# Output projection as seven half-size block products instead of one full product

## The chip, the cores and the metric

The kernel runs on one core of one Trainium2 chip. The metric is the device time of one execution in microseconds (us). The kernel before took 826.01 us as the median of 3 runs (825.94 to 826.08).

## The reference, cut to what matters

One transformer-like block on `x` of 512 rows by 2048 columns in fp32. The change touches the last line only; the rest explains what fills the engines before it.

```python
h    = rms_norm(x, norm_w)
proj = h @ w_in                                  # 2048 x 6144: q, k, v, gate_a, pool input, gate_p
attn = diff_attention(q, k, v, ...)              # 8 heads, two softmaxes each
pool = multiscale_pool(u_p, w_pool, pool_scale)  # four window sizes
mixed = concat([attn * silu(g_a), pool * silu(g_p)])   # 512 x 2048
x = x + mixed @ w_out                            # w_out is 2048 x 2048
```

## The kernel before, in words

The kernel feeds TensorE (PE) each fp32 factor as two `float32r` parts, a high one (ScalarE, ACT, copies and rounds) and a low one (VectorE, DVE, subtracts the high part from the fp32 value). A product is three matmuls: high*high, low*high, high*low (`products`, line 292 issues every one of them, so all have one line in the profile).

The first part of the kernel runs four rounds over the input projection with attention and pooling threaded between its 48 half-units a round. What it leaves in `mixed` is the transposed result: 16 k-tiles of 128 partitions (the contraction index) by 512 columns (the rows of x). The last values of `mixed` are written by DVE at lines 810 (head) and 836 (pool, announced by `pool_mixed`).

The output projection walks four column chunks of 512 of `w_out`. In a chunk each of 16 k-tiles is one "half" of 128x512 weights. SP loads two halves with one DMA into one of four slots of `raw` (`load_out`, line 181). ACT writes the high part of a half into one of four slots of `w_hi` (`split_high`, line 483, waits until PE has used the half four before, `w_used`), DVE writes the low part (`split_low`, line 669). PE then runs 12 matmuls on the half: four row tiles of x times three products, into four PSUM banks; two sets of four banks alternate between chunks. `mixed` itself is split once, a k-tile at a time, by ACT line 520 and DVE line 700, into `h_hi` and `h_lo`. After a chunk DVE adds the residual x (line 856, `add_x`) and SP stores the result (lines 249 to 262). The last four tiles are stored one at a time.

Every engine takes its instructions in the order of the program, so a wait on one holds all that follow on that engine. GpSimd (POOL) does nothing after its one broadcast at the start (line 269).

## Time and profile before

| what | value |
|---|---|
| median of 3 runs | 826.01 us (825.94 to 826.08) |
| span of the profiled execution | 824.4 us |
| PE busy | 802.7 us, 97% |
| DVE busy | 468.4 us, 57% |
| ACT busy | 364.6 us, 44% |
| POOL busy | 2.5 us |
| mean granted TensorE clock | 0.995 of full speed |
| DMA | 89.12 MB, mean 108 GB/s |

The profile covers one execution from its first to its last instruction (the span); the run's time is 1.6 us longer than the span. Busy shares of PE count overlapping pipelined matmuls, so the distance between the starts of matmuls says more than their durations. A line with "idle before" says how long the engine stood still ahead of such instructions and which engine released it.

### The profile page before, as it was taken

Reading aid. Unit: us, or ns where it says so; the run is one execution under the profiler, and the core shown is the slowest. Engines: PE = TensorE matmul, PEld = TensorE weight load, DVE = VectorE, ACT = ScalarE, POOL = GpSimd, SP = SyncE. Lnnn points to the kernel's source line nnn. Section 1 sums busy time; section 2 is a strip of 40 time slices with the busy share of each in tenths; the row PEclk is TensorE's granted clock in tenths of the full one; section 3 lists DMA queues with packets and bytes.
Section 4 is the critical chain, followed back from the end, with each engine's and each line's share of the span. In section 5 each row is a group of like instructions: output and inputs, shape, how many; then the busy total and the mean of one; then the engine's idle time right before and its main releaser. Section 6 shows DMA issues by size and latency. Waiting matters only on the chain.

```text
span 824.4 us, 10257 instructions
## 1 busy us (share of the span) xinstructions
PE 802.7 (97%) x3616; PEld 662.8 (80%) x3616; DVE 468.4 (57%) x694; ACT 364.6 (44%) x590; POOL 2.5 (0%) x5
## 2 busy tenths in 40 slices
PE   3799999999999999999999999999999999999998
PEld 3688888888888888888888888888888888888886
DVE  5628775772686667428775672686668643232322
ACT  6544445542454634454346543454644542222220
POOL 1000000000000000000000000000000000000000
PEclk9899999999999999999999999999999999999999
DMA  9233622213244222233622223254212464424331
GB/s 339 82 103 102 179 77 78 69 59 127 76 127 129 74 76 76 77 101 102 178 76 76 76 70 108 81 144 130 66 63 77 128 204 153 146 88 148 102 102 51
DMA packets 69525, 89.12 MB, mean 108 GB/s; under 512 B 4481, under 2 KB 53889, under 8 KB 68993
## 3 DMA queue, kind: packets, MB, share of 16 engines
q1 hardware_dynamic: 67632, 86.72, 33.8%
q10 hardware_dynamic: 1874, 2.18, 0.9%
q8 instruction: 9, 0.15, 0.1%
q14 instruction: 10, 0.08, 0.0%
HBM read 78.39 MB, written 4.19 MB: 100 GB/s over the span
## 4 chain that ended last, share of the span: by engine, by line
PE 96%; DVE 2%; ACT 1%; DMA 1%; issue 0%; DVEq 0%; ACTq 0%
PE ps L292 94%; PE ps L382 2%; DVE mixed L663 1%; DVE h_lo L653 1%; DMA mixed<-in_x 1%; ACT at_hi L468 0%; PE ps L354 0%; DVE mixed L856 0%; PE ps L284 0%; ACT h_hi L461 0%; ACT x_rms L471 0%; DVE x_rstd L662 0%; DVEq L852 0%; DVEq L661 0%; ACTq L466 0%
## 5 line engine op out<-in xcount | busy, mean ns | idle before, releaser
L669 DVE TENSOR_TENSOR w_lo<-raw,w_hi 128x512 fp32r<-128x512 f32 x256 | 175.5, 690 | 300.4 <-ACT w_hi L483 297.8
L483 ACT CAST w_hi<-raw 128x512 fp32r<-128x512 f32 x256 | 158.7, 622 | 374.0 <-PE ps L292 373.0
L292 PE MATMUL ps<-h_hi,w_hi 128*128 128x512 f32 x768 | 303.0, 395 | 1.8 <-DVE h_lo L653 1.8
L292 PE MATMUL ps<-h_lo,w_hi 128*128 128x512 f32 x768 | 300.4, 391 | 0.0
L292 PE MATMUL ps<-h_hi,w_lo 128*128 128x512 f32 x768 | 205.9, 390 | 0.0
L292 PEld LDWEIGHTS ps<-h_hi,w_hi 128*128 128x128 f32 x768 | 144.8, 189 | 31.8 <-ACT w_hi L483 2.2
L292 PEld LDWEIGHTS ps<-h_hi,w_lo 128*128 128x128 f32 x768 | 144.4, 188 | 30.6
L292 PEld LDWEIGHTS ps<-h_lo,w_hi 128*128 128x128 f32 x768 | 144.9, 189 | 29.6
L292 PE MATMUL ps<-w_hi,h_hi 128*128 128x512 f32 x256 | 99.7, 389 | 0.0
L292 PE MATMUL ps<-w_hi,h_lo 128*128 128x512 f32 x256 | 99.6, 389 | 0.0
L292 PE MATMUL ps<-w_lo,h_hi 128*128 128x512 f32 x256 | 99.6, 389 | 0.0
L292 PEld LDWEIGHTS ps<-w_hi,h_hi 128*128 128x128 f32 x256 | 48.1, 188 | 10.1 <-issue 0.3
L292 PEld LDWEIGHTS ps<-w_lo,h_hi 128*128 128x128 f32 x256 | 48.1, 188 | 10.0
L292 PEld LDWEIGHTS ps<-w_hi,h_lo 128*128 128x128 f32 x256 | 48.1, 188 | 10.0
L591 ACT ACTIVATE probs<-ps,neg_max 128x512 f32<-128x512 f32 x64 | 43.6, 691 | 0.0
L777 DVE TENSOR_REDUCE row_max<-ps 128x2 f32<-128x1024 f32 x32 | 38.9, 1217 | 0.0
L784 DVE TENSOR_TENSOR at_lo<-ps,at_hi 128x512 fp32r<-128x512 f32 x32 | 21.9, 684 | 10.0 <-ACT at_hi L584 10.0
L284 PE MATMUL ps<-ident,mixed 128*128 128x128 f32 x64 | 10.5, 330 | 15.8 <-DVE mixed L663 15.7
L292 PE MATMUL ps<-kh_twice,q_stack 128*128 128x512 f32 x64 | 25.4, 397 | 0.0
L292 PE MATMUL ps<-kl_twice,q_stack 128*128 128x512 f32 x64 | 24.9, 390 | 0.0
L765 DVE SCALAR_TENSOR_TENSOR probs<-probs,coef 128x512 f32<-128x512 f32 x32 | 24.0, 752 | 1.1
L584 ACT CAST at_hi<-ps 128x512 fp32r<-128x512 f32 x32 | 18.7, 583 | 10.5 <-PE ps L292 10.5
(105 smaller groups left out, 584.3 us busy)
## 6 DMA issues: line engine op xcount, KB each, us to landing
raw<-in_w_in SPq DMA_DIRECT2D x96, 512.0 KB, 3.6
raw<-in_w_out SPq DMA_DIRECT2D x32, 512.0 KB, 3.8
mixed<-in_x SPq DMA_DIRECT2D x8, 1024.0 KB, 6.9
out<-mixed SPq DMA_DIRECT2D x3, 1024.0 KB, 6.5
kh_twice<-kh_twice SPq DMA_DIRECT2D x8, 256.0 KB, 5.3
kl_twice<-kl_twice SPq DMA_DIRECT2D x8, 256.0 KB, 6.0
q_stack<-v_hi SPq DMA_DIRECT2D x8, 256.0 KB, 3.6
wp_raw<-in_w_pool ACTq DMA_DIRECT2D x4, 256.0 KB, 3.3
```

Of the source, the lines that this page charges most:

```text
L284: last = nc.tensor.transpose(ps[:, bank + i // 4, (i % 4) * P:(i % 4 + 1) * P], x_rows[:, t, (8 * b + i) * P:(8 * b + i + 1) * P], ident[: ...
L292: last = nc.tensor.matmul(dst, lhs, rhs, start=first and i == 0, stop=final and i == len(pairs) - 1, skip_group_check=True)
L382: last = nc.tensor.transpose(ps[:, TB, t * P:(t + 1) * P], probs[:, 0, t * P:(t + 1) * P], ident[:, :])
L483: nc.scalar.copy(w_hi[:, h % W_SLOTS, :], raw[:, unit % RAW_SLOTS, part * 512:part * 512 + 512]).then_inc(w_hi_ready, 1)
L584: nc.scalar.copy(at_hi[:, :, t * P:(t + 1) * P], ps[:, TB, :].rearrange("p (t s) -> p t s", t=ST)).then_inc(at_hi_ready, 1)
L591: nc.scalar.activation(probs[:, c, :], ps[:, S0 + c, :], ACT.Exp, bias=neg_max[:, c:c + 1], scale=SCALE, accum_out=row_sum[:, c:c + 1]).th ...
L653: nc.vector.tensor_tensor(h_lo[:, 8 * b:8 * b + 8, t * P:(t + 1) * P], ps[:, bank:bank + 2, :].rearrange("p b (k s) -> p (b k) s", s=P), h ...
L663: nc.vector.scalar_tensor_tensor(out=x_rows[:, t, :], in0=x_rows[:, t, :], scalar=x_rstd[:, t:t + 1], in1=norm_row, op0=ALU.mult, op1=ALU. ...
L669: nc.vector.tensor_tensor(w_lo[:, h % W_SLOTS, :], raw[:, unit % RAW_SLOTS, part * 512:part * 512 + 512], w_hi[:, h % W_SLOTS, :].bitcast( ...
L765: nc.vector.scalar_tensor_tensor(out=probs[:, 0, :], in0=probs[:, 1, :], scalar=coef[:, :], in1=probs[:, 0, :], op0=ALU.mult, op1=ALU.add) ...
L777: chain(nc.vector.reduce_max(row_max[:, :], ps[:, S0:S0 + 2, :], AX_X))
L784: nc.vector.tensor_tensor(at_lo[:, :, t * P:(t + 1) * P], ps[:, TB, :].rearrange("p (t s) -> p t s", t=ST), at_hi[:, :, t * P:(t + 1) * P] ...
```

## The change

The product is cut in 2x2 blocks: `mixed` in A(row, col) with 256 rows of x and 1024 of the contraction, `w_out` in B(row, col) of 1024 by 1024. Seven block products ("passes") replace the eight of the plain scheme. A pass has 8 k-tiles of weights 1024 columns wide, each taken in two halves of 512 columns, and 2 row tiles: 6 matmuls a half, 16 halves a pass, 112 halves in all.

| pass | form of A (left factor) | weights | banks |
|---|---|---|---|
| 0 | A00 | B00 (`wide`, plain load) | set 0, fresh |
| 1 | A10 - A11 | B00+B01 (`wide` += ) | set 1, fresh |
| 2 | A01 | B10 (`tall`, plain load) | set 0, added to pass 0 |
| 3 | A00 - (A10 - A11) | B00+B01+B11 (`wide` +=) | set 1, added to pass 1 |
| 4 | A00 - A10, in place | B01+B11 (`tall` load, then +=) | set 0, fresh |
| 5 | A01 - (A00 - A10 + A11) | B11 (`tall`, plain load) | set 1, fresh |
| 6 | A11 | B00+B01+B10+B11 (`wide` +=) | set 0, added to pass 4 |

The sums of weights are made by 32 DMAs of 512 KB that POOL issues with an accumulate operation (`accum_op`): they add a block of `w_out` in HBM to what lies in SBUF. Each waits until DVE has made the low part of that tile for the pass before. The sums of A are 16 `tensor_tensor` of 128x512 on POOL; another 12 on POOL add a shared corner term to the x blocks, or subtract it. SP makes 32 plain loads of `w_out` tiles of 512 KB, as before (8 `wide`, ahead of the passes, and 24 `tall`, within them), four loads of x blocks of 1 MB, three block stores of 1 MB and four of 256 KB. ACT and DVE split each of 112 halves, and each form of A in four pairs of k-tiles (28 pairs, 128x512 each; 16 before). ACT copies pass 0's banks once (4 instructions), DVE reads banks 24 times (16 before). To make room the buffers lie at fixed offsets in one arena: `tall` over the attention buffers, `wide_b` over `at_hi` and `at_lo`, the x blocks over the upper halves of `h_hi` and `h_lo`, `corner` and `form_sum` over `work`.

The added lines at the core of the diff; the removed ones are the loops told of above (lines 229 to 263, 425 to 449 and 848 to 865):

```diff
+        PASS_SET = (0, 1, 0, 1, 0, 1, 0)
+        PASS_FRESH = (True, True, False, False, True, True, False)
+        PASS_WIDE = (True, True, False, True, False, False, True)
+        PASS_LANDED = (16, 16, 16, 32, 16, 48, 48)
 ...
+            for h in range(PASSES * P_HALVES):
+                p, hj = divmod(h, P_HALVES)
+                j, part = divmod(hj, 2)
+                slot = h % W_SLOTS
+                if hj == 0 and p == 1:
+                    pe.wait_ge(evacuated, ROUNDS * 4 + START)
+                    pe.wait_ge(pool_mixed, ROUNDS * 2 + START)
+                if j % 2 == 0 and part == 0:
+                    pe.wait_ge(form_lo_ready, (KP // 2) * p + j // 2 + 1)
+                pe.wait_ge(w_lo_ready, IN_HALVES + h + 1)
+                for i in range(2):
+                    b = 2 * part + i
+                    bank = OUT_BANKS[PASS_SET[p]][b]
+                    if j == 0 and p == 2:
+                        pe.wait_ge(first_copied, b + 1)
+                    if j == 0 and p >= 3:
+                        pe.wait_ge(bank_read, 4 * (p - 3) + b + 1)
+                    hi, lo = form_tile(h_hi, p, j, i), form_tile(h_lo, p, j, i)
+                    last = products(ps[:, bank, :],
+                                    [(hi, w_hi[:, slot, :]), (lo, w_hi[:, slot, :]), (hi, w_lo[:, slot, :])],
+                                    j == 0 and PASS_FRESH[p], j == KP - 1)
+                    if j == KP - 1 and i == 0:
+                        last.then_inc(bank_done, 1)
+                last.then_inc(w_used, 1)
 ...
+            def form_high(p, pair):
+                if p == 0:
+                    act.wait_ge(w_used, IN_HALVES - G_HALVES + 2)
+                    act.wait_ge(head_mixed, 2 * pair + 2 + START)
+                elif p == 1:
+                    act.wait_ge(w_used, IN_HALVES - G_HALVES + 4)
                 else:
+                    act.wait_ge(w_used, p_halves(p - 2, KP - 1, 1))
+                if p == 2 or p == 6:
+                    act.wait_ge(pool_mixed, ROUNDS * 2 + START)
+                elif p > 0:
+                    act.wait_ge(form_summed, (KP // 2) * (0, 0, 0, 1, 2, 3)[p] + pair + 1)
+                nc.scalar.copy(form_pair(h_hi, p, pair), form_fp32(p, pair)).then_inc(form_hi_ready, 1)
+            def split_form_w(h):
+                p, hj = divmod(h, P_HALVES)
+                j, part = divmod(hj, 2)
+                if part == 0:
+                    act.wait_ge((wide_in, wide_added, tall_in, wide_added, tall_added, tall_in, wide_added)[p][j],
+                                PASS_LANDED[p])
+                act.wait_ge(w_used, IN_HALVES + h - W_SLOTS + 1)
+                nc.scalar.copy(w_hi[:, h % W_SLOTS, :], w_tile(p, j)[:, part * 512:part * 512 + 512]
+                               ).then_inc(w_hi_ready, 1)
 ...
+            form_high(0, KP // 2 - 1)
+            for h in range(W_SLOTS, PASSES * P_HALVES):
+                p, hj = divmod(h, P_HALVES)
+                split_form_w(h)
+                if hj in (4, 7, 10, 13) and p + 1 < PASSES:
+                    form_high(p + 1, (hj - 4) // 3)
+                if p == 1 and hj in (2, 3):
+                    for b in (2 * hj - 4, 2 * hj - 3):
+                        wait_bank(act, 0, b)
+                        nc.scalar.copy(corner_part(b), ps[:, OUT_BANKS[0][b], :]).then_inc(first_copied, 1)
 ...
+            def read_bank(p, b):
+                wait_bank(dve, p, b)
+                bank = ps[:, OUT_BANKS[PASS_SET[p]][b], :]
+                if p == 1 and b == 0:
+                    dve.wait_ge(x_part_in[2], 16)
+                if p == 2 and b == 0:
+                    dve.wait_ge(x_part_in[0], 16)
+                if p == 3:
+                    dve.wait_ge(first_copied, b + 1)
+                if p >= 4:
+                    dve.wait_ge(x_summed, 4 * (p - 4) + b + 1)
 ...
+            form_low(0, KP // 2 - 1)
+            for h in range(W_SLOTS, PASSES * P_HALVES):
+                p, hj = divmod(h, P_HALVES)
+                split_form_low(h)
+                if hj in (4, 7, 10, 13) and p + 1 < PASSES:
+                    form_low(p + 1, (hj - 4) // 3)
+                if p >= 2 and hj in (2, 3):
+                    for b in (2 * hj - 4, 2 * hj - 3):
+                        read_bank(p - 1, b)
+            for b in range(4):
+                read_bank(PASSES - 1, b)
 ...
+            sp.wait_ge(head_done, ROUNDS * 2)
+            for j in range(RAW_SLOTS, KP):
+                load_wide(j)
+            sp.wait_ge(pool_done, ROUNDS)
+            sp.wait_ge(w_used, IN_HALVES)
+            for p in range(PASSES):
+                for j in range(KP):
+                    if p == 0 or p == 1:
+                        if j % 2 == 1:
+                            sp.wait_ge(w_lo_ready, p_halves(p, j, 1))
+                            load_tall(4 * p + j // 2, 1, 0)
+                        if j == 2:
+                            load_x(1 - p, 0)
+                        if p == 1 and j == 6:
+                            load_x(1, 1)
+                    if p == 2:
+                        sp.wait_ge(w_lo_ready, p_halves(p, j, 1))
+                        load_tall(j, 0, 1)
+                    if p == 3 and j == 0:
+                        load_x(0, 1)
+                    if p == 3 and j == 2:
+                        store(0, 0, 2)
+                    if p == 4:
+                        sp.wait_ge(w_lo_ready, p_halves(p, j, 1))
+                        load_tall(j, 1, 1)
+                    if p == 5 and j == 2:
+                        store(1, 1, 4)
+                    if p == 6 and j == 2:
+                        store(0, 1, 5)
 ...
+            def add_wide(p, j, row, col):
+                pool.wait_ge(w_lo_ready, p_halves(p, j, 1))
+                pool.dma_start(w_tile(0, j), w_block(row, col, j), accum_op=ALU.add).then_inc(wide_added[j], 16)
+            for j in range(KP):
+                add_wide(0, j, 0, 1)
+                if j == 0:
+                    pool.wait_ge(pool_mixed, ROUNDS * 2 + START)
+                    pool.wait_ge(head_mixed, ROUNDS * 2 + START)
+                if j % 2 == 0:
+                    pair = j // 2
+                    nc.gpsimd.tensor_tensor(sum_of(pair), block_of(1, 0, pair), block_of(1, 1, pair), ALU.subtract
+                                            ).then_inc(form_summed, 1)
+            for j in range(KP):
+                add_wide(1, j, 1, 1)
+            for pair in range(KP // 2):
+                pool.wait_ge(form_lo_ready, KP // 2 + pair + 1)
+                nc.gpsimd.tensor_tensor(sum_of(pair), block_of(0, 0, pair), sum_of(pair), ALU.subtract
+                                        ).then_inc(form_summed, 1)
+            for pair in range(KP // 2):
+                nc.gpsimd.tensor_tensor(block_of(1, 0, pair), block_of(0, 0, pair), block_of(1, 0, pair), ALU.subtract
+                                        ).then_inc(form_summed, 1)
+            for j in range(KP):
+                pool.wait_ge(tall_in[j], 32)
+                pool.dma_start(tall[:, j, :], w_block(1, 1, j), accum_op=ALU.add).then_inc(tall_added[j], 16)
+            for pair in range(KP // 2):
+                pool.wait_ge(form_lo_ready, 3 * (KP // 2) + pair + 1)
+                nc.gpsimd.tensor_tensor(sum_of(pair), block_of(0, 1, pair), sum_of(pair), ALU.subtract
+                                        ).then_inc(form_summed, 1)
+            for j in range(KP):
+                add_wide(3, j, 1, 0)
+            for row, col in ((1, 1), (0, 1), (1, 0)):
+                pool.wait_ge(x_part_in[2 * row + col], 16)
+                if (row, col) == (1, 0):
+                    pool.wait_ge(bank_read, 4)
+                for b in range(4):
+                    pool.wait_ge(bank_read, 8 + b + 1)
+                    nc.gpsimd.tensor_tensor(x_part(row, col, b), x_part(row, col, b), corner_part(b),
+                                            ALU.subtract if row > col else ALU.add).then_inc(x_summed, 1)
```

## Rows read from the trace of the kernel before

**Rows 1.** The page: busy time, its share of the span, instructions of each engine.
```profile
PE 802.7 (97%) x3616; PEld 662.8 (80%) x3616; DVE 468.4 (57%) x694; ACT 364.6 (44%) x590; POOL 2.5 (0%) x5
```

**Rows 2.** The chain that ended last, shares of the span by engine and line.
```profile
PE 96%; DVE 2%; ACT 1%; DMA 1%; issue 0%; DVEq 0%; ACTq 0%
PE ps L292 94%; PE ps L382 2%; DVE mixed L663 1%; DVE h_lo L653 1%; DMA mixed<-in_x 1%; ACT at_hi L468 0%; PE ps L354 0%; DVE mixed L856 0%; PE ps L284 0%; ACT h_hi L461 0%; ACT x_rms L471 0%; DVE x_rstd L662 0%; DVEq L852 0%; DVEq L661 0%; ACTq L466 0%
```

**Rows 3.** Groups by line, 644 to 820 us (count | busy us, mean ns | idle before).
```profile
L292 PE MATMUL ps<-w_hi,h_hi 128*128 128x512 f32 x256 | 99.7, 389 | 0.0
L669 DVE TENSOR_TENSOR w_lo<-raw,w_hi 128x512 fp32r<-128x512 f32 x62 | 42.9, 691 | 106.6 <-ACT w_hi L483 106.6
L483 ACT CAST w_hi<-raw 128x512 fp32r<-128x512 f32 x61 | 38.0, 622 | 120.7 <-PE ps L292 120.7
```

**Rows 4.** Timeline of PE, first and late output matmuls (start us, duration us).
```profile
645.98 0.47 PE L292 MATMUL ps<-w_hi,h_hi 128*128 128x512 f32 x1
...
811.99 0.39 PE L292 MATMUL ps<-w_hi,h_hi 128*128 128x512 f32 x1
...
818.79 0.39 PE L292 MATMUL ps<-w_hi,h_hi 128*128 128x512 f32 x1
...
819.93 0.39 PE L292 MATMUL ps<-w_lo,h_hi 128*128 128x512 f32 x1
```

**Rows 5.** Timeline of DVE and SP at the end.
```profile
818.38 2.66 DVE L856 TENSOR_TENSOR mixed<-ps,mixed 128x512 f32<-128x512 f32 x4 [7.56 <-PE ps L292]
819.10 2.31 SPq L261 DMA_DIRECT2D out<-mixed  x4
```

**Rows 6.** Timeline of DVE where the projection starts.
```profile
645.97 0.69 DVE L700 TENSOR_TENSOR h_lo<-mixed,h_hi 128x512 fp32r<-128x512 f32 x1
646.57 0.69 DVE L669 TENSOR_TENSOR w_lo<-raw,w_hi 128x512 fp32r<-128x512 f32 x1
647.18 1.40 DVE L836 SCALAR_TENSOR_TENSOR mixed<-ps,p_scale,work 128x512 f32<-128x512 f32 x2
```

**Rows 7.** Timeline of ACT where the projection starts.
```profile
643.77 0.61 ACT L520 CAST h_hi<-mixed 128x512 fp32r<-128x512 f32 x1
644.29 0.62 ACT L483 CAST w_hi<-raw 128x512 fp32r<-128x512 f32 x1
644.81 1.02 ACT L621 ACTIVATE work<-ps 128x1024 f32<-128x1024 f32 x1
```

**Rows 8.** POOL's arithmetic in the whole trace, by line (count | busy us, mean ns | idle before).
```profile
L269 POOL PARTITION_BROADCAST work<-work x1 | 2.3, 2293 | 2.1 <-DMA work<-in_norm_w 2.1
L915 POOL MEMSET const-float32-1.0<- 128x1 f32 x1 | 0.1, 99 | 0.0
```

**Rows 9.** SP's issues of w_out loads: ns min/median/max, first and last start.
```profile
L181 SPq DMA_DIRECT2D raw<-in_w_out x32: 367/372/383, 611.5 to 789.1; - x32
```

**Rows 10.** Stretches: us, busy us of PE, PEld, DVE, ACT, POOL; granted clock, DMA share, GB/s.
```profile
6.00:12.00 6.00, 1.09 (x5) 1.10 (x6) 3.63 (x4) 4.46 (x6) 0.00 (x0) 1.00 1.01 424
649.70:655.10 5.40, 5.40 (x25) 4.50 (x24) 2.59 (x4) 2.24 (x5) 0.00 (x0) 1.00 0.86 275
```

**Rows 11.** DMA issues by line (queue, count, KB each, median us from issue to landing).
```profile
raw<-in_w_out SPq DMA_DIRECT2D x32, 512.0 KB, 3.8
kh_twice<-kh_twice SPq DMA_DIRECT2D x8, 256.0 KB, 5.3
```

**Rows 12.** Stretches after PE's idle time near the start, columns as in rows 10.
```profile
26.00:28.00 2.00, 0.30 (x2) 0.00 (x0) 2.00 (x3) 1.67 (x3) 0.00 (x0) 0.50 0.00 0
28.00:30.00 2.00, 1.88 (x5) 1.50 (x6) 2.00 (x3) 1.67 (x2) 0.00 (x0) 0.50 0.00 0
```

**Rows 13.** Timeline of PE in the second of these stretches.
```profile
29.57 0.63 PE L292 MATMUL ps<-h_lo,w_hi 128*128 128x512 f32 x1
30.00 0.63 PE L292 MATMUL ps<-h_hi,w_hi 128*128 128x512 f32 x1
```

More of the change, by code:

```diff
@@ new lines, in hybrid_block, with fixed @@
+        at0 = -(-nc.sbuf_base // 64) * 64
+        sb("arena", [P, at0 - nc.sbuf_base + ARENA], U8)
+        place = [at0]
+        def fixed(name, shape, dt=F32, at=None):
+            offset = place[0] if at is None else at
+            size = 4
+            for n in shape[1:]:
+                size *= n
+            if at is None:
+                place[0] += size
+            return nc.alloc_sbuf_tensor_at(name, shape, dt, offset=offset), offset
+        h_hi, h_hi_at = fixed("h_hi", [P, KT, SEQ], F32R)
@@ L767, in dve_round @@
                                                        op0=ALU.mult, op1=ALU.add).then_inc(attn_ready, 1)
-                    split_low(m + 3, r)
+                    if last_round and m + 3 >= HALVES:
+                        split_form_low(m + 3 - HALVES)
+                    else:
+                        split_low(m + 3, r)
                     if m in (40, 45):
```

231 lines of the change are left out of this document (112 added, 119 removed).

## The prediction

> **What bounds the kernel now.** I read the page's busy times first. PE is at work 97% of the span, DVE 57%, ACT 44%, POOL is empty [rows 1]. Busy PE is not yet bound PE, so the chain of waits comes next: 94% of the time that leads to the end is one line, 292, the matmuls [rows 2]. The groups of the projection's stretch then say who waits for whom: ACT stood idle 120.7 us for PE and DVE 106.6 us for ACT, while the matmuls show no idle time [rows 3]. So PE alone sets the pace of the output projection, and everything else has room there.
>
> What one matmul costs is read from starts, not durations, because they overlap: from 811.99 to 818.79 there are 30 starts, so 6.80 / 30 = 0.2267 us each. The whole projection agrees: 768 matmuls start from 645.98 to 819.93, 173.95 / 767 = 0.2268 us [rows 4]. Its weights are loaded beside it; each matmul of the new scheme has the same shape and the same pair of load and product, so I keep 0.2267. For DVE and ACT the distance of starts counts too: 646.57 - 645.97 = 0.60 us on DVE [rows 6] and 644.29 - 643.77 = 0.52 us on ACT [rows 7] for a 128x512 operation.
>
> **What is removed.** 768 matmuls become 7 x 16 x 6 = 672. The 96 that go are worth 96 x 0.2267 = 21.8 us, all on the path. A half now lasts 6 x 0.2267 = 1.36 us and a pass 16 halves, 21.8 us.
>
> **ACT and DVE.** A pass asks ACT for 16 splits and 4 forms, 20 x 0.52 = 10.4 us (pass 1 has 4 copies more, 12.5). It asks DVE for 16 + 4 + 4 bank reads, 24 x 0.60 = 14.5 us. Both fit in 21.8. The splits run up to four halves ahead: half h is split when h-4 is done, about 1.1 us later it is ready, and PE wants it three halves (4.1 us) after the start of that; the lead is 3 us. Cost 0; PE's pace hides it. With that cover gone (a DVE held for over 3 us) each us shows in full.
>
> **Start and end.** The round before is unchanged, and the four plain `wide` tiles loaded as late as the last attention product are first split some 10 us later: 0. At the end the last four banks are read by DVE one after the other and stored in four DMAs of 256 KB as before: DVE's four reads begin at 818.38, beside the last matmuls, and the issues follow at 819.10 [rows 5]. The new last half ends bank by bank in the same way; 0, at most 0.7 us either way (a row tile more or less behind PE).
>
> **The sums of A on POOL: the chain through pass 0.** This is the place where a wait is added. ACT takes the form of pass 1 pair by pair after halves 4, 7, 10 and 13 of pass 0, in order, and holds all later weight splits until POOL has made the pair's sum. POOL makes it in order too, between its DMA issues: sum 1 stands behind the add of tile 2, sum 2 behind tile 4, sum 3 behind tile 6, and each add waits until DVE has finished that tile's second half (halves 5, 9, 13). So a ring closes: split, DVE, POOL issue I, POOL sum S, ACT form, split. In us from PE's first output matmul: the last pool values are there at 2.6 (line 836 starts at 647.18 and takes 1.40 [rows 6]). Half 5 is ready at 2.6 + S + 0.52 + 0.52 + 0.60; half 9 I + S + 3 x 0.52 + 0.60 later; half 13 I + S + 4 x 0.52 + 0.60 later; half 14 I + S + 2 x 0.52 + 0.60 later. Sum: 2.6 + 4S + 3I + 11 x 0.52 + 4 x 0.60 = 10.7 + 4S + 3I, and some 12 hand-overs that I estimate at 0.1 us each, 11.9 + 4S + 3I. PE wants half 14 at 14 x 1.36 = 19.0. Loss: 4S + 3I - 7.1.
>
> The trace shows neither S nor I. For S the ends are DVE's 0.60 us of the same shape [rows 6] and POOL's one real instruction, 2.29 us for a much larger output [rows 8]; I take the middle, 1.5. For I they are SP's issue, 0.37 us [rows 9], and again 2.29 us of POOL work for software that prepares one DMA; I take 1.0, nearer to SP's, since it is the same kind of job. Loss 6.0 + 3.0 - 7.1 = 1.9 us; ends 0 and 4 x 2.29 + 3 x 2.29 - 7.1 = 8.9.
>
> Later forms have a pass of slack: the sums for pass 3 start when the last add of pass 1 is issued, some 4 us ahead of pass 2, and are wanted one by one from 1.4 us into it. But in pass 2 POOL makes eight sums in a row.
>
> **POOL beside DVE.** Nothing runs on POOL in the projection now, so the trace shows no case of the two at once [rows 8], and from the rows alone each might run at its own pace: cost 0. If they exclude one another, pass 2 has 8 x 1.5 + 14.5 = 26.5 us of work for 21.8 plus the lead of 3, a loss of 1.7; other passes have 6 + 14.5 = 20.5, none. I take 0.6. By the Trainium skill, "SBUF — State Buffer", section "Who interferes with whom", a VectorE instruction with two SBUF inputs (the low parts are such) and a GpSimd one that reads SBUF keep each other out for the whole instruction; by that rule the sum would carry the 1.7 instead, and no run here shows it yet.
>
> **The accumulating DMAs.** The traffic of the projection grows by 32 x 512 KB. Plain price: at full use of the DMA engines the trace moves 424 GB/s [rows 10], so 512 KB take 1.25 us; the old loads of 2 KB rows reached 275 GB/s at a share of 0.86, or 320 GB/s, 1.6 us [rows 10]. The new rows are 4 KB, so 1.25. Within the passes: 24 `tall` loads 30 us, x blocks 4 x 2.5 = 10, two of the stores 5 by the time the last weights are due: 45 us. The 32 adds cost 32A. The last tile is due at about 6 x 21.8 + 19.0 - 4 = 146 us, so the queues keep up as a whole up to A = 101 / 32 = 3.15; up to the last tile of pass 4, 24A + 32.5 against 4 x 21.8 + 15 gives 2.9. No row shows an accumulating DMA. Lower end: the plain 1.25 us. Upper ends: 3.8 us if a DMA's whole issue-to-landing time repeated one by one, and 5.3 us, that of an SBUF-to-SBUF copy of half the size [rows 11]. An add must read both HBM and SBUF and write once, so I take twice the plain load, 2.5 us: nothing is late, cost 0. By the Trainium skill, "Collectives: The Full Stack", section "The bandwidth ceiling: the fold count and why AG ≠ RS ≠ AR", a DMA reduction runs at about half a copy's rate (ratio 1.93) because of its second source read; an estimate by it is 2.4 us, and the sum stays.
>
> **Sum.** Span 824.4 - 21.8 + 1.9 + 0.6 = 805.1 us. The runs last 1.6 us more than the span, so 806.7; I say 807. The median (826.01) and the span plus 1.6 are the same number here. Own range with small errors of each term: 804 to 812.
>
> **Rivals.**
> A. The adds are slow, and the DMA engines become the bound. For it: 16.8 MB of read-modify-write by an operation that no row prices, ends of 3.8 and 5.3 us. Against: nothing but the argument of two reads. Price: the work past 146 us shows, 45 + 32A - 146. It eats the gain of 19.3 at A = 3.76, the point from which the kernel is slower. At 4.55 (the middle of the upper ends) 44.6 us late: 826 - 19.3 + 44.6 = 851. At 5.3: 875. Place: waits of ACT's w_hi on the added tiles from pass 1 or 3 on, worst in passes 5 and 6. POOL's queue makes it worse, if issues wait for earlier ones to drain: the x sums that DVE needs in pass 5 stand behind the last eight adds.
> B. POOL is slow (S 2.29, I 1.6) but DMAs keep up. For it: software on the path. Against: only one instruction of it in the trace. Ring of pass 0: 9.2 + 4.8 - 7.1 = 6.9. Exclusion in pass 2: 18.3 + 14.5 - 24.8 = 8.0. Together 14.9, so 826 - 21.8 + 14.9 = 819; stalls of over 2 us may also cost clock: after idle time near the start PE was granted 0.50, its 1.2 GHz level [rows 12], and matmuls started 0.43 us apart [rows 13], so 4 us at that level lose 1.9 us.
> C. Both small losses meet and the gain is gone, 825 to 828.
>
> **Chances.** Forecast 0.50, B 0.20, A 0.25, C 0.05. What a measurement can tell from no change is about 0.2%, 1.7 us. Faster: forecast and B, 0.70; C is mostly within, 0.03; slower A and the rest, 0.27. The range for 8 in 10 begins at 803 (no loss at all is 804 and a little for the tail) and reaches through B to the milder half of A, 840; the likeliest case alone is 804 to 812.
>
> **What would show it.** The changed profile should have 3520 matmuls of the same 0.23 us distance, so a projection of about 155 us. Right about pass 0: idle time of ACT at the form copies (form_high) on POOL of 1 to 3 us each, and of PE before half 14. Right about the adds: issue-to-landing times near 4 to 6 us, no idle time of w_hi on a DMA. Wrong: landings over 10 us, DMA share near 1 for most of the projection, ACT waiting on `raw` or `tall` (rival A); POOL busy over 15 us a pass, or DVE's distances grown while POOL works (rival B). The prediction fails if A is over 3.8 us, or if POOL's sum and issue together take over 5.

## The result, and the profile after

The changed kernel took 832.97 us (median of 4, 831.21 to 837.57) where the kernel before took 825.98 (median of 4, 825.86 to 826.08): a ratio of 1.0093, 95% interval 1.0074 to 1.0113. It is 0.9% slower. I had forecast 807, faster with a chance of 0.7. The profiled execution is the longest of the four, 837.57 us with a span of 835.7: 11.3 more than before, where the medians differ by 7.0. What follows accounts for that one execution, and the sizes of its terms are its own.

The page's busy times come first, to stand against [rows 1], then its chain (against [rows 2]) and three of its DMA lines (count, KB each, median us from issue to landing):

```profile
PE 787.1 (94%) x3520; PEld 647.2 (77%) x3520; DVE 541.1 (65%) x762; ACT 401.7 (48%) x654; POOL 65.6 (8%) x65
...
PE 89%; DVE 6%; issue 2%; ACT 1%; POOL 1%; DMA 0%; ACTq 0%; DVEq 0%
...
tall<-in_w_out SPq DMA_DIRECT2D x24, 512.0 KB, 8.0
raw<-in_w_out POOLq DMA_DIRECT2D x12, 512.0 KB, 12.8
wide_b<-in_w_out POOLq DMA_DIRECT2D x12, 512.0 KB, 18.9
```

The 96 matmuls are gone (3520, as foreseen), but PE's share of the chain fell from 96% to 89% and DVE's rose from 2% to 6%. DVE has 72.7 us more of busy time for 68 more instructions: far more than 0.6 us each (0.6 would make 41 us). The groups of the projection, 646 to 830 us, show where (against [rows 3]; the low parts are line 867 now):

```profile
L424 PE MATMUL ps<-w_hi,h_hi 128*128 128x512 f32 x222 | 88.7, 399 | 24.9 <-DVE w_lo L867 17.2 <-issue 7.7
L867 DVE TENSOR_TENSOR w_lo<-tall,w_hi 128x512 fp32r<-128x512 f32 x48 | 56.8, 1192 | 18.1 <-ACT w_hi L670 17.5
L670 ACT CAST w_hi<-tall 128x512 fp32r<-128x512 f32 x48 | 29.9, 623 | 52.5 <-PE ps L424 52.5
```

PE, which stood idle nowhere in [rows 3], now waits 24.9 us, mostly for DVE's low part, whose mean went from 691 to 1192 ns. ACT's split is unchanged (622 and 623) and waits for PE, not for a DMA. A mean hides what kind of slowness it is, so the timelines of POOL and DVE are laid beside each other at the two longest stops. POOL in pass 2 (start us, duration us):

```profile
693.82 0.87 POOL L362 DMA_DIRECT2D wide_b<-in_w_out  x1 [1.73 <-DVE w_lo L867]
694.38 5.32 POOL L378 TENSOR_TENSOR form_sum<-mixed,form_sum 128x512 f32<-128x512 f32 x4
699.33 5.22 POOL L381 TENSOR_TENSOR mixed<-mixed 128x512 f32<-128x512 f32 x4
```

DVE in the same stretch:

```profile
692.76 0.69 DVE L867 TENSOR_TENSOR w_lo<-wide_b,w_hi 128x512 fp32r<-128x512 f32 x1 [0.61 <-ACT w_hi L670]
694.18 12.13 DVE L867 TENSOR_TENSOR w_lo<-tall,w_hi 128x512 fp32r<-128x512 f32 x3 [0.72 <-ACT w_hi L670]
```

PE in the same stretch:

```profile
697.12 0.39 PE L424 MATMUL ps<-w_lo,h_hi 128*128 128x512 f32 x1
705.21 0.77 PE L424 MATMUL ps<-w_hi,h_hi 128*128 128x512 f32 x1 [7.70 <-issue]
705.77 0.63 PE L424 MATMUL ps<-w_hi,h_lo 128*128 128x512 f32 x1
706.20 0.63 PE L424 MATMUL ps<-w_lo,h_hi 128*128 128x512 f32 x1
```

POOL in pass 4:

```profile
753.97 0.87 POOL L362 DMA_DIRECT2D wide_b<-in_w_out  x1 [1.49 <-DVE corner L1033]
754.53 10.17 POOL L400 TENSOR_TENSOR x_right<-x_right,corner 128x512 f32<-128x512 f32 x8
764.38 5.18 POOL L400 TENSOR_TENSOR x_left<-x_left,corner 128x512 f32<-128x512 f32 x4
```

DVE in the same stretch:

```profile
755.54 14.58 DVE L867 TENSOR_TENSOR w_lo<-tall,w_hi 128x512 fp32r<-128x512 f32 x1
770.04 0.68 DVE L859 TENSOR_TENSOR h_lo<-form_sum,h_hi 128x512 fp32r<-128x512 f32 x1
```

One DVE instruction that takes 0.69 us elsewhere lasts 14.58 us: from just after POOL's run of twelve sums begins until it ends. In pass 2, three instructions last 12.13 us together beside a run of eight; they start 0.60 apart once they are free, so the first was held for 10.9. A third stop of the kind, 5.07 us at 738.95, lies beside four sums in pass 3. PE runs on for the lead that it has and then stops: 697.12 to 705.21 is 8.09 us where the pitch is 0.23, so 7.9 lost; 757.60 to 770.26 loses 12.4; the third, 1.9. Together 22.2 us.

The two longest stops also cost clock. The stretches (columns as in [rows 10]) around the first:

```profile
700.00:702.00 2.00, 0.00 (x0) 0.00 (x0) 2.00 (x1) 0.00 (x0) 2.00 (x3) 0.88 1.06 279
702.00:704.00 2.00, 0.00 (x0) 0.00 (x0) 2.00 (x1) 0.00 (x0) 2.00 (x3) 0.50 1.04 281
706.00:708.00 2.00, 2.00 (x6) 1.52 (x6) 2.00 (x4) 0.00 (x0) 0.00 (x0) 0.50 1.04 268
```

After the stop PE works at 0.50, its 1.2 GHz level, and its matmuls start 0.43 us apart, as at the start of the kernel before [rows 12, 13], until 708.3. The stop of 12.4 us is followed by the same, until 773.3; after the one of 1.9 us the granted clock stays at 1.00. The starts at 0.50 come 3.0 us late in sum. With smaller delays elsewhere, the starts that came late without being a stop add up to 4.1 us over the projection.

The span is then accounted for. The first output matmul starts at 649.24 instead of 645.98 (+3.3); the matmuls save 21.8; pass 0 has stops of 1.3, 0.8 and 1.5 us (+3.6); the three stops behind DVE are +22.2; the late starts +4.1; the time after the last matmul is 0.1 shorter. Sum +11.3, the difference of the spans.

The extra 3.3 us are there before any changed work. POOL at the start of this kernel:

```profile
9.32 2.30 POOL L357 PARTITION_BROADCAST work<-work  x1 [8.88 <-issue]
```

And of the kernel before:

```profile
2.49 2.29 POOL L269 PARTITION_BROADCAST work<-work  x1 [2.05 <-DMA work<-in_norm_w]
```

### The profile page after: what moved, and what is told of

It is laid out like the page before. It is cut to its first block, busy times and chain, and to the rows that moved or that the text cites. A ratio compares the mean times of both kernels' runs of the same rounds, so it can differ in the third digit from the quotient of the medians.

```text
span 835.7 us, 10145 instructions
## 1 busy us (share of the span) xinstructions
PE 787.1 (94%) x3520; PEld 647.2 (77%) x3520; DVE 541.1 (65%) x762; ACT 401.7 (48%) x654; POOL 65.6 (8%) x65
## 3 DMA queue, kind: packets, MB, share of 16 engines
q0 software_dynamic: 4608, 16.78, 10.3%
## 4 chain that ended last, share of the span: by engine, by line
PE 89%; DVE 6%; issue 2%; ACT 1%; POOL 1%; DMA 0%; ACTq 0%; DVEq 0%
PE ps L424 87%; DVE w_lo L867 3%; PE ps L514 2%; DVE mixed L822 1%; DVE h_lo L812 1%; PE ps L486 0%; DVE h_lo L859 0%; POOL form_sum L371 0%; ACT h_hi L660 0%; DMA work<-in_norm_w 0%; POOL work L357 0%; PE ps L416 0%; DVE corner L1033 0%; ACT at_hi L602 0%; ACT w_hi L670 0%
## 5 line engine op out<-in xcount | busy, mean ns | idle before, releaser
L828 DVE TENSOR_TENSOR w_lo<-raw,w_hi 128x512 fp32r<-128x512 f32 x192 | 131.2, 690 | 192.8 <-ACT w_hi L617 190.2
L617 ACT CAST w_hi<-raw 128x512 fp32r<-128x512 f32 x192 | 118.8, 622 | 250.7 <-PE ps L424 249.7
L424 PE MATMUL ps<-w_hi,h_hi 128*128 128x512 f32 x224 | 89.4, 399 | 24.9 <-DVE w_lo L867 17.2
L424 PE MATMUL ps<-w_lo,h_hi 128*128 128x512 f32 x224 | 88.2, 394 | 0.0
L424 PE MATMUL ps<-w_hi,h_lo 128*128 128x512 f32 x224 | 88.2, 394 | 0.0
L867 DVE TENSOR_TENSOR w_lo<-tall,w_hi 128x512 fp32r<-128x512 f32 x48 | 56.8, 1192 | 18.1 <-ACT w_hi L670 17.5
L362 POOL DMA_DIRECT2D raw<-in_w_out x12 | 11.3, 1189 | 640.4 <-DVE w_lo L867 640.4
L670 ACT CAST w_hi<-tall 128x512 fp32r<-128x512 f32 x48 | 29.9, 623 | 52.5 <-PE ps L424 52.5
L424 PEld LDWEIGHTS ps<-w_lo,h_hi 128*128 128x128 f32 x224 | 42.6, 190 | 9.1
L867 DVE TENSOR_TENSOR w_lo<-wide_b,w_hi 128x512 fp32r<-128x512 f32 x32 | 25.8, 825 | 10.5 <-ACT w_hi L670 10.1
L867 DVE TENSOR_TENSOR w_lo<-raw,w_hi 128x512 fp32r<-128x512 f32 x32 | 23.5, 744 | 10.4 <-ACT w_hi L670 10.4
```

The source lines that it names most:

```text
L362: pool.dma_start(w_tile(0, j), w_block(row, col, j), accum_op=ALU.add).then_inc(wide_added[j], 16)
L424: last = nc.tensor.matmul(dst, lhs, rhs, start=first and i == 0, stop=final and i == len(pairs) - 1, skip_group_check=True)
L617: nc.scalar.copy(w_hi[:, h % W_SLOTS, :], raw[:, unit % RAW_SLOTS, part * 512:part * 512 + 512]).then_inc(w_hi_ready, 1)
L670: nc.scalar.copy(w_hi[:, h % W_SLOTS, :], w_tile(p, j)[:, part * 512:part * 512 + 512]).then_inc(w_hi_ready, 1)
L828: nc.vector.tensor_tensor(w_lo[:, h % W_SLOTS, :], raw[:, unit % RAW_SLOTS, part * 512:part * 512 + 512], w_hi[:, h % W_SLOTS, :].bitcast( ...
L867: nc.vector.tensor_tensor(w_lo[:, h % W_SLOTS, :], w_tile(p, j)[:, part * 512:part * 512 + 512], w_hi[:, h % W_SLOTS, :].bitcast(F32), ALU ...
```

## The experiments

**Is it the sums or the DMAs?** The DMA engines are full in the stretches above (share 1.04 to 1.06), landings are two to three times what I had foreseen, and the sums run beside all that. The first kernel keeps the 32 adds and leaves out the 28 sums on POOL (left factors and x parts are taken unsummed, so that part of the computation is left out).

```diff
-   nc.gpsimd.tensor_tensor(sum_of(pair), block_of(1, 0, pair), block_of(1, 1, pair), ALU.subtract).then_inc(form_summed, 1)
...
-   return (block_of(0, 0, pair), sum_of(pair), block_of(0, 1, pair), sum_of(pair), ...)[p]
+   return (block_of(0, 0, pair), block_of(1, 0, pair), block_of(0, 1, pair), block_of(0, 0, pair), ...)[p]
```

> Leaves out all 28 elementwise operations of POOL (the sums of A's blocks and the corner term on x); the forms of A are taken from plain blocks instead, so the output is not the reference's. The 32 accumulating DMAs, all other DMAs and all work of PE, ACT and DVE stay. Theory (DVE's low parts, which read two SBUF operands, are held for as long as POOL runs elementwise operations back to back): all long stalls go. What is left against the kernel before is -21.8 us of matmuls and +3.4 us of a later start, so 806 to 810 us, and no DVE operation of the projection over 1 us. Rival (the full DMA engines, share near 1.0 from pass 0 to pass 5, hold DVE or PE): the stalls stay in good part, 818 us or more, and ACT or DVE wait for DMAs.

It took 803.82 us (802.51 to 803.92), ratio 0.9731 (0.9714 to 0.9747), span 800.7: 2 us below the expected range, which had kept the late start. A stretch of its projection, columns as in [rows 10]:

```profile
672.00:694.00 22.00, 22.00 (x99) 18.23 (x98) 15.56 (x24) 12.29 (x22) 4.33 (x5) 1.00 1.05 276
```

Its landings:

```profile
raw<-in_w_out POOLq DMA_DIRECT2D x12, 512.0 KB, 17.1
wide_b<-in_w_out POOLq DMA_DIRECT2D x12, 512.0 KB, 21.7
```

The DMA share is 1.05 to 1.06 through 650 to 738 us, the adds land even later than in the changed kernel, and PE is never idle (22.00 of 22.00). Full DMA engines with landings of 22 us cost nothing here: rival A falls. The broadcast is back at 3.36 us, so the late start belongs to the sums too.

**The same sums on DVE.** All the work of the change, with the 28 sums moved to DVE, one after every third half, so that POOL only issues.

```diff
-   nc.gpsimd.tensor_tensor(sum_of(pair), block_of(1, 0, pair), block_of(1, 1, pair), ALU.subtract).then_inc(form_summed, 1)
...
+   nc.vector.tensor_tensor(sum_of(pair), block_of(1, 0, pair), block_of(1, 1, pair), ALU.subtract).then_inc(form_summed, 1)
...
+   if p == 0 and hj in (5, 8, 11):
+       make_sum(1, (hj - 2) // 3)
+   if hj in (5, 8, 11, 14):
+       if p in (1, 2, 3):
+           make_sum(p + 2, (hj - 5) // 3)
+       if p >= 4:
+           sum_x(*((1, 1), (0, 1), (1, 0))[p - 4], (hj - 5) // 3)
```

> Full computation. The same 28 sums are made by DVE, one after every third half, POOL only issues the accumulating DMAs. DVE has then at most 28 operations of 0.60 us in a pass of 21.8 us, 17 us. Theory: 806 to 811 us. Rival (DMA engines): 818 us or more. A third possibility is that DVE is too full for its lead of about 3 us: then PE shows short stalls at halves 5, 8, 11 and 14 and the time is 811 to 818 us.

804.03 us (802.43 to 804.25), ratio 0.9727 (0.9711 to 0.9743), span 802.2: faster than both kernels, 2.7% under the one before. Its first output matmul starts at 645.81, not late, and the time is 2 us below the range expected. Its groups of the low parts and of ACT's splits of `tall`:

```profile
L838 DVE TENSOR_TENSOR w_lo<-tall,w_hi 128x512 fp32r<-128x512 f32 x48 | 33.1, 689 | 12.7 <-ACT w_hi L641 11.6
L641 ACT CAST w_hi<-tall 128x512 fp32r<-128x512 f32 x48 | 29.8, 623 | 29.7 <-PE ps L395 27.3 <-DMA tall<-in_w_out 2.4
```

The low part takes 689 ns where it took 1192. The span of before less the matmuls is 824.4 - 21.8 = 802.6; this kernel has 802.2. The whole saving is there once POOL does no arithmetic, with 28 more DVE instructions hidden under PE. ACT waits 2.4 us for a DMA, which reaches nobody.

**The sums on POOL, but spread.** Each sum on POOL waits for a half of DVE, so that no two should be adjacent.

```diff
+   def make_sum(p, pair, half):
...
+       if half > 0:
+           pool.wait_ge(w_lo_ready, IN_HALVES + half + 1)
...
+   at(p, 3 * q + 5, 0, make_sum(p + 2, q, P_HALVES * p + 3 * q + 5))
...
+   at(4 + n, 3 * q + 5, 0, sum_x(row, col, q, P_HALVES * (4 + n) + 3 * q + 5))
```

> Full computation. The 28 sums stay on POOL, but none follows another at once: each waits until DVE has finished a given half, one every third half; the last eight accumulating DMAs are issued a little later. Theory in its narrow form (it is the back-to-back run that starves DVE, one sum costs DVE at most 1.6 us): 807 to 813 us, DVE operations of at most 2.3 us, nearly no PE stall. Rival form (any POOL operation beside DVE costs the projection its whole length, 28 x 1.6 = 45 us, less the room DVE has): 820 us or more. Rival DMA: 820 us or more.

815.85 us (814.73 to 816.5), ratio 0.9872 (0.9855 to 0.9888). Right in direction, some 3 us above the expected range. Its trace shows three causes. The broadcast starts at 10.21 and the first output matmul at 650.07, 4.1 us late, which I had not counted. And POOL ran late in pass 4, so the waits had passed by the time it came to them, and three sums stood right behind an issue (PE stopped for 3.0 us), as POOL's timeline shows:

```profile
754.43 0.87 POOL L362 DMA_DIRECT2D wide_b<-in_w_out  x1 [2.88 <-issue]
755.00 4.05 POOL L396 TENSOR_TENSOR x_right<-x_right,corner 128x512 f32<-128x512 f32 x3
```

DVE in the same stretch:

```profile
754.79 5.41 DVE L884 TENSOR_TENSOR w_lo<-tall,w_hi 128x512 fp32r<-128x512 f32 x2 [1.58 <-ACT w_hi L687]
```

The third is smaller. From pass 3 on some single sums, too, stood between two issues. Beside two of those one DVE instruction took 3.46 us (at 717.93), where 2.3 at most was expected, and PE stopped for 0.8 us. With a stop of 0.6 us later and one of 1.1 us in pass 0, all stops add up to 5.4 us.

**Does a long run alone hold DVE?** The kernel before, with runs on POOL over spare memory, after a wait each: 4 and 12 sums, 12 copies, 12 fills, then 12 single sums.

```diff
+   def run(half, count, op):
+       pool.wait_ge(w_lo_ready, IN_HALVES + half + 1)
...
+               ins = nc.gpsimd.tensor_tensor(spare[n], probs[:, 0, :], probs[:, 1, :], ALU.subtract)
...
+   run(13, 4, "two")
+   run(19, 12, "two")
+   run(32, 12, "one")
+   run(42, 12, "none")
+   for h in range(50, 62):
+       run(h, 1, "two")
```

> The kernel before, with extra POOL work on spare SBUF during the projection: a run of 4 and a run of 12 tensor_tensor (two SBUF inputs), a run of 12 copies (one SBUF input), a run of 12 memsets (no input), and 12 single tensor_tensor, one after each of halves 50 to 61. No accumulating DMA and DMA share under 0.5. Theory: the run of 12 holds one DVE low part for about 12 x 1.6 - 1 = 18 us while add_x (one PSUM and one SBUF input) goes on at 0.68 us; the run of 4 holds one for 5 to 6 us; a single one costs under 1.6 us; memsets hold nothing; copies, which read SBUF too, hold it as well. PE loses what exceeds a lead of three halves of 2.72 us: 18 - 8 = 10 us for the run of 12, nothing for the run of 4. Total 836 to 850 us depending on the copies. Rival (DMA load is what stretches DVE): every DVE operation stays under 1 us and the time is 826 us.

This missed. 830.84 us (2 runs), ratio 1.0057 (1.0037 to 1.0077), and all of the 4.0 us of span are the start (broadcast at 10.00, first output matmul at 650.00). The run of twelve on POOL:

```profile
695.26 14.79 POOL L280 TENSOR_TENSOR work<-probs 128x512 f32<-128x512 f32 x10 [9.99 <-DVE w_lo L693]
```

DVE in the same stretch:

```profile
699.93 1.38 DVE L693 TENSOR_TENSOR w_lo<-raw,w_hi 128x512 fp32r<-128x512 f32 x1 [1.57 <-ACT w_hi L507]
702.70 1.54 DVE L693 TENSOR_TENSOR w_lo<-raw,w_hi 128x512 fp32r<-128x512 f32 x1 [1.40 <-ACT w_hi L507]
705.37 1.83 DVE L693 TENSOR_TENSOR w_lo<-raw,w_hi 128x512 fp32r<-128x512 f32 x1 [1.12 <-ACT w_hi L507]
```

Here the two engines take turns: a DVE instruction waits for at most one of POOL's (up to 1.83 us instead of 0.69), and gets in before the next. The copies, with one input, brought DVE to 0.92 at most; the fills did nothing; `add_x`, whose one input is PSUM, took 2.48 us for four beside the run, undisturbed. So "POOL's run holds DVE" was too simple: something else in the changed kernel makes the difference. What differed there was, among other things, in-place operands, full DMA engines, and a DMA issue right before the run.

**In place, or the DMA load?** The kernel without sums, with four runs of six sums of spare data: in pass 2 not in place with the DMA engines full; in pass 3 in place; in pass 5 not in place and in pass 6 in place, both with the DMA engines nearly idle.

```diff
+   run(2, 1, False)
+   run(3, 8, True)
+   run(5, 8, False)
+   run(6, 4, True)
```

> The kernel of e1 (all 28 sums left out, so the output is not the reference's) with four runs of six back-to-back tensor_tensor on POOL over spare SBUF: after half 1 of pass 2 to a third place (out of place), after half 8 of pass 3 in place (the result over the second input), both while the DMA engines are full; after half 8 of pass 5 out of place and after half 4 of pass 6 in place, both with the DMA engines nearly idle. The probe in the kernel before held no DVE operation over 1.9 us, the changed kernel's runs held one for the whole run. Theory P (in place is what keeps DVE out between two operations): the runs of pass 3 and 6 hold a DVE low part for about 7 us each, those of pass 2 and 5 never over 1.9 us; PE loses about 3 us twice. Theory D (full DMA engines keep it out): the runs of passes 2 and 3 hold DVE for about 7 us, the others not. If all four hold it, it is something the two share with the changed kernel (the software queue in use, or the 2 x 256 shape), if none does, it is the kind of operand or the wait between them.

817.86 us (one run). The runs of passes 2, 5 and 6 took turns with DVE (in pass 2 four sums took 6.58 us, and DVE up to 1.78 for one instruction). That of pass 3 held it, as POOL's timeline shows:

```profile
729.20 0.88 POOL L387 DMA_DIRECT2D tall<-in_w_out  x1 [2.91 <-DMA tall<-in_w_out]
729.76 5.33 POOL L376 TENSOR_TENSOR form_sum<-probs,form_sum 128x512 f32<-128x512 f32 x4
734.72 2.79 POOL L376 TENSOR_TENSOR gate<-probs,gate 128x512 f32<-128x512 f32 x2
```

DVE in the same stretch:

```profile
729.65 9.03 DVE L857 TENSOR_TENSOR w_lo<-wide_b,w_hi 128x512 fp32r<-128x512 f32 x2 [0.72 <-ACT w_hi L660]
```

In place alone does not hold (pass 6), full DMA engines alone do not (pass 2). Pass 3 alone has two things: both of these at once, and a wait that had passed, so that the run stood right behind a DMA issue, as at all three stops of the changed kernel. The runs behind an issue, further down, tell these two apart.

**What an add costs the DMA engines.** The kernel without sums, the 32 adds as plain loads of the same rows.

```diff
-   pool.dma_start(w_tile(0, j), w_block(row, col, j), accum_op=ALU.add)
+   pool.dma_start(w_tile(0, j), w_block(row, col, j))
```

> The kernel of e1 with the accumulate operation taken off the 32 DMAs that POOL issues: plain loads of the same rows to the same places by the same queue (the weights of passes 1, 3, 4 and 6 are then single blocks; the output is not the reference's). It prices the accumulate: by the rule of two reads the queue's share of the 16 engines falls from 10.6% to 5 or 6% and the landings from 17 to 22 us to under 8 us; if an accumulating DMA costs no more than a plain one, both stay. The span stays at 801 us either way, since nothing waits for them.

802.42 us (one run), against 802.51 of the profiled run with adds: no difference in time. The queue of these DMAs (packets, MB, share of 16 engines), with adds:

```profile
q0 software_dynamic: 4608, 16.78, 10.6%
```

And with plain loads:

```profile
q0 software_dynamic: 4608, 16.78, 5.6%
```

0.106 x 800.7 / 32 = 2.65 us of all DMA engines an add, 0.056 x 800.5 / 32 = 1.40 a plain load, a ratio of 1.9. Both are the time that the packets took beside the other loads, at a DMA share of 1.05 with adds and 0.86 to 0.98 without. Landings fell to 7.5 to 8.5 us, the issue on POOL from 0.87 to 0.53.

**The start.** The kernel before with a single sum on POOL, late in the projection.

```diff
+   pool.wait_ge(w_lo_ready, IN_HALVES + 32)
+   nc.gpsimd.tensor_tensor(gate[:, 0, :], probs[:, 0, :], probs[:, 1, :], ALU.subtract)
```

> The kernel before with a single tensor_tensor of 128x512 on POOL, on spare SBUF, late in the projection. All three kernels with such operations on POOL so far began the broadcast of norm_w at 9.3 to 10.2 us, all without at 2.5 to 3.4 us, with or without software DMAs. Theory (a program that has an elementwise operation on POOL starts its first POOL work 7 us late): the broadcast begins near 10 us, PE's first projection matmul 3.3 to 4.0 us later than before, 829.3 to 830.0 us. Rival (the delay grows with the amount of POOL work or comes with chance): 826 us, broadcast at 2.5 us.

828.93 us (828.16 to 832.02, 7 runs) against 825.42, 3.5 us more, ratio 1.0051 (1.0035 to 1.0066). The broadcast starts at 10.31 instead of 2.49, the first output matmul at 648.67, 2.7 us late. One sum, which runs at 726.59, is enough to delay POOL's first real work by 7.8 us. In all kernels with sums on POOL the broadcast starts between 9.3 and 10.7 us; in those with software DMAs alone it does not come late (3.36, 2.77 and 2.65).

**Behind an issue, or not.** The kernel without sums, four runs of six sums, none in place (`run` waits for a half, issues a DMA if its last word is True, and makes six sums): behind a wait (pass 2), right behind an adding DMA issue, right behind a plain 256 KB issue (pass 5), behind a wait (pass 6). The third was meant to find the DMA engines idle.

```diff
+   run(2, 1, False)
...
+   add_wide(3, KP - 1, 1, 0)
+   for n in range(6):
...
+       nc.gpsimd.tensor_tensor(spare[n], source, other, ALU.subtract).then_inc(probed, 1)
+   run(5, 2, True)
+   run(6, 4, False)
```

> The kernel of e1 (all 28 sums left out) with four runs of six out-of-place tensor_tensor on POOL over spare SBUF. First, pass 2, behind a wait; second directly behind the issue of the last accumulating DMA of pass 3; third, pass 5 with the DMA engines nearly idle, directly behind the issue of a plain DMA of 256 KB into spare SBUF; fourth, pass 6, behind a wait. In e4 three runs behind a wait let DVE in after each operation, in place or not and with full or idle DMA engines, and the one directly behind a DMA issue did not. Theory Q (a run that follows POOL's own DMA issue without a pause keeps DVE's low part out until it ends): the second and third hold one DVE operation for 6 to 8 us and POOL's operations follow every 1.27 us, the first and fourth hold none over 1.9 us and follow every 1.6 to 1.7 us. Rival (in place after all, with e4's pass 6 an exception): none of the four holds it. If the second does and the third not, it takes an accumulating DMA or full DMA engines.

823.29 us (one run). The two runs behind an issue held DVE and the two behind a wait did not, as the theory has it; no run was in place, so that rival falls. The third, on POOL:

```profile
767.67 0.61 POOL L377 DMA_DIRECT2D head_out<-in_w_out  x1 [5.99 <-DVE w_lo L865]
768.30 4.99 POOL L379 TENSOR_TENSOR form_sum<-probs 128x512 f32<-128x512 f32 x4
773.24 2.48 POOL L379 TENSOR_TENSOR gate<-probs 128x512 f32<-128x512 f32 x2
```

DVE in the same stretch:

```profile
768.38 7.90 DVE L865 TENSOR_TENSOR w_lo<-tall,w_hi 128x512 fp32r<-128x512 f32 x1
```

The stretch (columns as in [rows 10]) beside it:

```profile
768.00:774.00 6.00, 3.30 (x15) 2.41 (x13) 6.00 (x2) 2.39 (x4) 5.98 (x6) 1.00 1.06 252
```

Behind the adding issue DVE was held for 8.54 us, beside the two runs behind waits it never took over 1.78 us. But the DMA engines were not idle at the third run, as the expectation had it: their share is 1.06. So a plain issue is enough, an adding one is not needed. Every run that held DVE, here and in the other kernels, had full DMA engines beside it (1.04 to 1.06). Full engines alone do not hold it (1.05 beside the runs behind waits in pass 2); whether an issue before the run does it with idle ones was not tried.

**The changed kernel with three waits.** A wait between the last DMA issue and each long run of sums (the eight, the four and the twelve on x), nothing else.

```diff
+   pool.wait_ge(w_lo_ready, p_halves(2, 0, 1))
...
+   pool.wait_ge(w_lo_ready, p_halves(3, 6, 1))
...
+   pool.wait_ge(w_lo_ready, p_halves(4, 2, 0))
```

> Full computation: the changed kernel with three waits more on POOL, each between its last accumulating-DMA issue and the run of sums that followed it at once (on a half of DVE's work one to two halves later; the third on half 4 of pass 4). Theory Q: the three holds of 12.1, 5.1 and 14.6 us go; DVE and POOL alternate, which still gives DVE only one operation per 1.7 us while a run lasts, so the run of 12 costs PE some 3 to 6 us; 812 to 820 us, no DVE operation over 2 us (the halves of a run seen apart). Rival (the runs of the real sums starve DVE whatever stands before them): 829 to 836 us as now.

829.2 us (827.81 to 830.91), ratio 1.0046 (1.003 to 1.0063): above the 812 to 820 expected, and inside the range of the rival, by which the real sums hold DVE whatever stands before them. The trace speaks against that rival at two of the three places. The first two waits did their work (sums mostly 1.7 us apart, DVE up to 1.78), the third had passed when POOL came to it, and there the hold stayed, as POOL's timeline shows:

```profile
751.96 0.88 POOL L362 DMA_DIRECT2D wide_b<-in_w_out  x1 [2.42 <-DVE w_lo L870]
752.52 10.15 POOL L403 TENSOR_TENSOR x_right<-x_right,corner 128x512 f32<-128x512 f32 x8
```

DVE in the same stretch:

```profile
752.12 16.57 DVE L870 TENSOR_TENSOR w_lo<-tall,w_hi 128x512 fp32r<-128x512 f32 x2 [0.42 <-ACT w_hi L673]
```

**The third wait moved seven halves on.**

```diff
-   pool.wait_ge(w_lo_ready, p_halves(4, 2, 0))
+   pool.wait_ge(w_lo_ready, p_halves(4, 5, 1))
```

> Full computation: e8 with its third wait moved from half 4 to half 11 of pass 4. In e8 half 4 had long been reached when the last accumulating DMA was issued (DVE was on half 9), so the run of 12 x sums still followed the issue at once and held a DVE low part for 16 us. Theory Q: behind a real wait DVE gets its turn after every operation; no DVE operation takes over 2 us, and of the 16 us held at least half comes back: 815 to 821 us against 829.2. Rival (a run of twelve in-place sums is too long whatever precedes it): 827 to 831 us, the hold stays.

819.38 us (819.21 to 819.87), ratio 0.9924 (0.9907 to 0.994). The x sums on POOL:

```profile
755.55 13.20 POOL L403 TENSOR_TENSOR x_right<-x_right,corner 128x512 f32<-128x512 f32 x8 [2.56 <-DVE w_lo L870]
768.70 7.01 POOL L403 TENSOR_TENSOR x_left<-x_left,corner 128x512 f32<-128x512 f32 x4
```

DVE in the same stretch:

```profile
759.02 1.78 DVE L862 TENSOR_TENSOR h_lo<-form_sum,h_hi 128x512 fp32r<-128x512 f32 x1
760.73 8.57 DVE L870 TENSOR_TENSOR w_lo<-tall,w_hi 128x512 fp32r<-128x512 f32 x5
```

The same twelve sums now take 20.2 us instead of 15.0, and DVE's instructions 1.7 us each instead of one of 14.58. Three waits took 832.97 to 819.38, 13.6 us, and turned the change from a loss into a gain. The span is still 15.1 us over that of the kernel with the sums on DVE: 3.2 are the late start, 3.3 the stops of pass 0, and most of the other 8.6 the turns that DVE loses.

## Why the prediction was wrong, step by step

**Matmuls, -21.8.** Right. The version with the sums on DVE has a span of 802.2, where 824.4 - 21.8 is 802.6.

**ACT and DVE, 0.** Right while DVE is left alone: no stop of PE in the first two experiments, though one of them puts 28 more instructions on DVE.

**The adds, 2.5 us each, 0.** Right: 2.65 measured, under the 2.9 to 3.15 that I had worked out as free, and nothing waited. My signs for rival A were not right, though: I had named landings over 10 us and a DMA share near 1 as signs of it. Both came, and cost nothing; the third sign, ACT waiting for `raw` or `tall`, did not come. Long landings (17 and 22 us in the first experiment, with no stop of PE) do not say that someone waits; that is read from the idle time of `w_hi`. By the Trainium skill, "Collectives: The Full Stack", section "The bandwidth ceiling: the fold count and why AG ≠ RS ≠ AR", a copy runs at 1.93 times the rate of a reduction, measured there on collectives. The 1.9 of these two kernels agrees.

**The ring of pass 0, +1.9.** The mechanism was right, the size low: 3.6. Both prices were close: a sum behind an issue lasts 1.6 us (1.5 taken) and an issue 0.87 (1.0 taken), so 4S + 3I - 7.1 gives 1.9 again. What is left fits the first sum, which starts at 653.99, 4.75 us after PE's first output matmul. I had its input ready at 2.6, and DVE had in fact written it by 2.1. POOL came 2.6 us later, and why was not tested (see what stays open).

**The start, 0.** Wrong: +3.3 in this kernel, 2.7 in the trace of the run with a single sum and 3.5 between its medians. I looked at what the sums displace in the projection, and not at what a kind of instruction that the program did not have before does to it elsewhere.

**"POOL beside DVE", 0.6 (1.7 if they exclude one another).** This is the step that failed. My span was 805.1 and the profiled one is 835.7; the 30.6 us between them are 22.2 - 0.6 of stops here, 4.1 of late starts (3.0 of them at the low clock behind the two longest stops), 3.3 of the start, 1.7 of pass 0, less 0.1 at the end. I had added up work: 26.5 us of POOL and DVE for 24.8 of room. That sum assumes that the two take turns, so that DVE falls behind slowly and PE's lead of 3 us covers it. The runs show two regimes. Behind a wait they do take turns, 1.7 us a turn, and the loss is near what I had foreseen: with three waits, pass 2 has stops of 1.0 and 0.9 us and late starts of 0.8, 2.7 in all, where I had 1.7. Right behind a DMA issue of POOL, DVE gets nothing until the run ends, and then what counts is not the sum but the longest run: the eight sums of pass 2 last 10.2 us, and less my lead of 3 that is a stop of 7.2 (7.9 measured); the twelve of pass 4 last 15.0, less 3 a stop of 12.0 (12.4 measured). Even without knowing the regime, the longest run should have been held against the lead. And I gave a run of eight to pass 2 alone and four sums to every other pass; the twelve sums on x that follow one another in pass 4 stand in no term. My conditions for failing were an add of over 3.8 us and a sum and issue of over 5 together; neither came (2.65, and 1.6 + 0.87), and the prediction failed by a step that I had given no such sign.

By the Trainium skill, "SBUF — State Buffer", section "Who interferes with whom", a VectorE instruction with two SBUF inputs and a GpSimd one that reads SBUF keep each other out for the whole instruction. The traces behind a wait agree one instruction at a time (DVE loses at most 1.1 us, where a sum alone lasts 1.3), and in its exceptions: the `add_x` with a PSUM input and POOL's fills disturbed nobody. That a whole run behind an issue shuts DVE out goes beyond it, and beside that rule the measurement decides.

**The rivals.** B had the right pair of engines and the remark that stops may cost clock, as the two longest did. Its price of 8.0 for pass 2 lies next to the 7.9 measured by chance: it gave POOL slow sums (2.29; they start 1.25 apart), and it, too, added work instead of looking for the longest run. The sums were faster than forecast and the harm larger. A was refuted by the first experiment. That 833 lies within my wide range of 803 to 840 is luck as well: the part above 828 was there for the milder cases of slow adds.

**What stays open.** Why an issue right before the run makes the difference, and whether it needs full DMA engines beside it. The length of the sums is not the reason. In the changed kernel they last 1.6 us behind an issue and overlap, since they start some 1.24 apart. In the run behind a plain issue they last 1.3 us and start 1.24 apart, as sums behind a wait do while DVE asks for nothing (1.29 and 1.25), and DVE was shut out all the same.

What POOL does before its first work was not tested either, but the trace has a hint. The row of the first sum's line in the changed kernel, two instructions of POOL's sequencer at 645.0 (ns min/median/max, first and last start):

```profile
L371 POOLq MODIFY_POOL_CONFIG  x2: 335/335/335, 645.0 to 645.0; - x2
```

The kernels without sums on POOL have one such pair of instructions, ahead of the broadcast, which starts 1.7 to 2.6 us later. Those with sums have a second pair ahead of the first sum. In them the broadcast starts 8.3 to 9.7 us after the first pair, and in the changed kernel the first sum 9.0 us after the second, though its input was ready 2.6 us earlier. A change of what POOL has loaded would fit both delays; no run tests it.

## What to carry to other kernels

Where an engine gets work beside one that may be shut out by it, hold the longest unbroken run against the lead of whoever waits, and not the sum of both against the time of the stage. If GpSimd both issues DMAs and computes, put a wait that really blocks between the issue and the arithmetic, look in the trace whether it did block, or give the arithmetic to an engine with room: here VectorE took all 28 sums for nothing, 804 us instead of 833. Full DMA engines and long landings are no finding until someone is seen to wait.

## What the runs showed of the hardware

- A run of 128x512 fp32 `tensor_tensor` on GpSimd right behind its own DMA issue (adding or plain) kept a VectorE instruction with two SBUF inputs out for the whole run: 5.07 us beside four sums, 7.90 and 8.54 beside six, 14.58 beside twelve. The DMA engines were full each time (share 1.04 to 1.06); idle ones were not tried. Behind a wait, runs of 4 to 12 let VectorE in each time, at most 1.83 us, with full DMA engines or not.
- One such instruction on GpSimd, 700 us into the program, moved its first work from 2.5 to 10.3 us and made this kernel 3.5 us longer (9.3 to 10.7 us in all kernels with sums on GpSimd); software DMAs alone did not.
- GpSimd's 128x512 fp32 subtraction takes 1.28 to 1.29 us alone and 1.25 from start to start, VectorE's 0.69 and 0.60.
- An adding DMA of 512 KB in 4 KB rows takes 2.65 us of all 16 DMA engines, a plain one 1.40, each measured beside other loads; its issue on GpSimd takes 0.87 us, a plain one 0.53.
